# Long convolutions of a three-layer block: tables in two stored parts, the input's factor in the filter, products on VectorE alone, first turning among the last gate tiles

## What is computed

```python
def bidirectional_long_conv(z, h_fwd, h_bwd):
    L, C = h_fwd.shape
    circ = jnp.concatenate([h_fwd, jnp.zeros((1, C), jnp.float32), h_bwd[:0:-1]], axis=0)
    hf = jnp.fft.rfft(circ, axis=0)
    zf = jnp.fft.rfft(z.astype(jnp.float32), n=2 * L, axis=1)
    y = jnp.fft.irfft(zf * hf[None], n=2 * L, axis=1)[:, :L]
    return y.astype(z.dtype)
...
    filters = implicit_filters(S, filt_w1, filt_b1, filt_w2, filt_b2, filt_w3, filt_b3, filt_w4, filt_freq)
    z = v
    for o, gate_o in enumerate((x1, x2)):
        z = gate_o * (bidirectional_long_conv(z, filters[:, o, 0], filters[:, o, 1]) + filt_bias[o] * z)
    y_hy = z * jax.nn.silu(g_hy)
```

## Time and profile before

| what | value |
|---|---|
| three runs | 4669.88, 4673.32, 4674.02 us (median 4673.32) |
| the profiled execution | 4672.72 us, its span 4670.9 us |
| mean granted clock of PE | 0.958 |
| busy share of the span: PE, DVE, ACT, POOL | 90%, 49%, 30%, 5% |
| chain that ended last: PE, DVE, ACT, DMA | 80%, 12%, 4%, 1% |
| last gate tile ends, merge's first matmul | 4125.3 us, 4420.66 us |

### The profile page before, as it was taken

One profiled execution on the slowest core, in us unless ns is written; L12 is line 12 of the kernel. 1 busy time (PEld: TensorE's weight loads), 2 busy tenths in 40 slices (PEclk: granted clock), 3 DMA queues, 4 the chain that ended last, 5 costly groups with the idle time before them and its releaser, 6 DMA issues.

```text
span 4670.9 us, 47189 instructions
## 1 busy us (share of the span) xinstructions
PE 4223.0 (90%) x18908; PEld 3155.9 (68%) x18908; DVE 2277.0 (49%) x3345; ACT 1398.0 (30%) x2292; POOL 231.6 (5%) x205
## 2 busy tenths in 40 slices
PE   6888889899999988889899999959999999987695
PEld 3566555688888766655578888847777777866574
DVE  6677346544343355355533332343445455466645
ACT  2323435322122233335321121123434333122221
POOL 2200000000000000000000000010000000021101
PEclk9999999899999989999899999979999999998897
DMA  4432200132331200200122221111111111122231
GB/s 163 153 111 84 83 14 1 45 99 91 92 98 55 81 28 23 84 14 1 32 77 68 72 68 54 46 63 46 41 46 41 46 41 59 46 90 77 90 135 45
DMA packets 87905, 304.16 MB, mean 65 GB/s; under 512 B 9735, under 2 KB 10535, under 8 KB 86600
## 3 DMA queue, kind: packets, MB, share of 16 engines
q1 hardware_dynamic: 69112, 229.31, 15.1%
q0 software_dynamic: 18576, 71.84, 4.9%
HBM read 266.50 MB, written 34.60 MB: 64 GB/s over the span
## 4 chain that ended last, share of the span: by engine, by line
PE 80%; DVE 12%; ACT 4%; issue 2%; DMA 1%; POOL 0%; SPq 0%; DVEq 0%; ACTq 0%
PE PS L915 54%; PE PS L1774 3%; PE PS L698 2%; PE PS L2793 2%; PE PS L1248 1%; PE PS L1646 1%; PE PS L2207 1%; PE PS L1501 1%; PE PS L1495 1%; PE PS L1675 1%; PE PS L2234 1%; PE PS L1645 1%; PE PS L2220 1%; PE PS L626 1%; DVE WL L471 1%
## 5 line engine op out<-in xcount | busy, mean ns | idle before, releaser
L915 PE MATMUL PS<-hi,WH 128*128 128x512 f32 x2816 | 1170.8, 416 | 111.2 <-issue 37.6
L915 PE MATMUL PS<-lo,WH 128*128 128x512 f32 x2816 | 1131.5, 402 | 0.0
L915 PE MATMUL PS<-hi,WL 128*128 128x512 f32 x2816 | 1126.1, 400 | 0.0
L915 PEld LDWEIGHTS PS<-hi,WH 128*128 128x128 f32 x2816 | 539.3, 192 | 292.2 <-issue 106.0
L915 PEld LDWEIGHTS PS<-hi,WL 128*128 128x128 f32 x2816 | 538.9, 191 | 131.5
L915 PEld LDWEIGHTS PS<-lo,WH 128*128 128x128 f32 x2816 | 540.4, 192 | 120.2 <-issue 5.4
L465 ACT ACTIVATE WH<-raw 128x1024 fp32r<-128x1024 f32 x304 | 319.8, 1052 | 793.4 <-PE PS L915 601.1
L471 DVE TENSOR_TENSOR WL<-raw,WH 128x1024 fp32r<-128x1024 f32 x304 | 391.1, 1287 | 260.6 <-ACT WH L465 260.5
L915 PE MATMUL PS<-al,WH 128*128 128x512 f32 x1024 | 408.6, 399 | 0.0
L915 PE MATMUL PS<-ah,WH 128*128 128x512 f32 x1024 | 403.5, 394 | 0.0
L915 PE MATMUL PS<-ah,WL 128*128 128x512 f32 x1024 | 401.4, 392 | 0.0
(11 more groups left out here) (423 smaller groups left out, 5465.9 us busy)
## 6 DMA issues: line engine op xcount, KB each, us to landing
adab<-in_w_ada POOLq DMA_DIRECT2D x120, 512.0 KB, 4.6
raw<-in_win SPq DMA_DIRECT2D x104, 512.0 KB, 3.6
raw<-in_up SPq DMA_DIRECT2D x64, 512.0 KB, 3.6
raw<-in_down SPq DMA_DIRECT2D x64, 512.0 KB, 3.6
raw<-in_dft SPq DMA_DIRECT2D x24, 512.0 KB, 3.7
sp_x<-X SPq DMA_DIRECT2D x24, 512.0 KB, 6.3
X<-sp_x SPq DMA_DIRECT2D x24, 512.0 KB, 5.4
raw<-in_wout SPq DMA_DIRECT2D x24, 512.0 KB, 3.7
```

Source lines behind the costliest of these rows:

```text
L915: mm = pe.matmul(bank[b + hf], w[:, k, :], r[:, k, HALF[hf]], start=k == 0 and w is wh and r is hi, stop=k == 7 and w is wl)
```

## The change

Code around it is in the kernel's own words, with the lines of the kernel before where there are any.

1. `dft` and `idft` tables lie in HBM as two arrays each, high and low part (`two_parts`, on the host). SP loads both (a second DMA of 512 KB for each of the 40 table tiles), ACT copies both (`WH` and `WL`), and `weights_dve` skips table tiles.
2. `fbias` is added to the filter's value at position 0 (one DMA of 1x1024, two additions of 1x512 on DVE), so L2706 goes away and the gate multiplies the PSUM bank at once.
3. All products and all eight `Yf` rows run on DVE; POOL only loads `cb`. `zc` has one buffer instead of two, `p1` is new.
4. The first turning (`o` = 0) runs on banks 6 and 7 during the last three gate tiles; `zh`, `zl` moved to memory that is free by then. For `o` = 1, four of the eight groups are turned among the tiles of the inverse.
5. The first spectrum block takes both tables' even halves before the odd ones. Inverse and spectrum use other banks, so that each starts without the other's being drained.
6. The merge splits `Yb` before the last inverse has ended.

```diff
-HYENA = rest_at(20) + 10
+HYENA = rest_at(20)
+SPECTRUM = 6.3
+ORDER = 98.5
 def turned_at(o, nt):
-    return HYENA + 175 * o + 1.5 * nt
+    if o == 0:
+        return rest_at(17) + 4 * nt
+    return inverse_at(0, 1, nt + 1) + 0.6 if nt < 4 else HYENA + ORDER + (3.0 if nt < 6 else 5.75) + 0.4 * (nt % 2)
...
-MERGE = HYENA + 360
+MERGE = inverse_at(1, 1, 4)
...
                 sp.dma_start(halves(to) if key[0] == "wout" else to, source(key)).then_inc(*W_RAW[j % 2].next(j, by=16))
+                if is_table(j):
+                    to, src = table_low(j)
+                    if j > 7 and not is_table(j - 2):
+                        sp.wait_ge(*DA_DVE["pair", 3])
+                        sp.wait_ge(*GH_OUT[1][71])
+                    sp.dma_start(to[:, :], src).then_inc(*W_RAW[j % 2].next(j, by=16))
...
                 act.activation(WH[:, j % 2, :], raw[:, j % 2, :], ACT.Copy).then_inc(*W_HI.next(j))
+                if is_table(j):
+                    act.activation(WL[:, j % 2, :], table_low(j)[0][:, :], ACT.Copy).then_inc(*W_TABLE.next(j))
...
             for j in range(len(WEIGHTS)):
+                if is_table(j):
+                    continue
...
                         dve.tensor_tensor(m.ft[0:1, o, :], PS[0:1, 6 + o, :], m.dec[0:1, 0, :],
-                                          ALU.mult).then_inc(*FI_DVE.next("value", (0, 0, o)))
+                                          ALU.mult).then_inc(*FI_DVE.next("middle", o))
+                        dve.wait_ge(*FI_DVE["middle", o])
+                        dve.wait_ge(*FBIAS_IN[0])
+                        dve.tensor_tensor(m.ft[0:1, o, :], m.ft[0:1, o, :], m.fso[0:1, 0, o, :],
+                                          ALU.add).then_inc(*FI_DVE.next("value", (0, 0, o)))
...
-                    pool.tensor_tensor(PROD, z0, csn, ALU.mult).then_inc(*HY_POOL.next("cross", o, mt))
...
+                    dve.tensor_tensor(m.p1[:, :, :], z1, imag, ALU.mult).then_inc(*HY_DVE.next("minus", (o, mt)))
+                    dve.tensor_tensor(m.p2[:, :, :], z0, imag, ALU.mult).then_inc(*HY_DVE.next("cross", (o, mt)))
...
-                        dve.scalar_tensor_tensor(out=zp, in0=zp, scalar=vc("fbias", 4 * o + ct), in1=bank[4 * par + ct],
-                                                 op0=ALU.mult, op1=ALU.add).then_inc(*HY_DVE.next("biased", o, par, ct))
-                        dve.wait_ge(*HY_DVE["biased", o, par, ct])
-                        dve.tensor_tensor(zp, zp, gp, ALU.mult).then_inc(*HY_DVE.next("filtered", o, par, ct))
+                        dve.tensor_tensor(zp, bank[inverse_bank(o, par, ct)], gp, ALU.mult).then_inc(
+                            *HY_DVE.next("filtered", o, par, ct))
...
+def two_parts(table):
+    part, power = np.frexp(table)
+    high = np.ldexp(np.round(part * 2048) / 2048, power)
+    return np.stack([high, table - high]).astype(np.float32)
```

More of the change, by code:

```diff
@@ L537, in setup_sp @@
             sp.dma_start(m.w4[:, :, :, :].rearrange("p a b c -> p (a b c)"), D["fw4"]).then_inc(*W4_IN.next(0, by=16))
+            sp.dma_start(m.fso[0:1, 0, :, :], D["fbias"]).then_inc(*FBIAS_IN.next(0, by=16))
             yield 2.0
@@ L2514, in turned_pe @@
                             pe.wait_ge(*RE_DVE["conv", 4 + i])
+                        pe.wait_ge(*DA_ACT["out", 11, 1])
+                        pe.wait_ge(*DA_DVE["turned", BLOCKS - 1])
                     if o:
                         pe.wait_ge(*HY_DVE["filtered", 0, par, 3])
-                    if nt % 4 > 1:
+                    if nt % 4 > 1 or nt > 3 and not o:
                         pe.wait_ge(*HY_DVE["low", o, nt - 2])
[L2519 to L2522, removed]
                     for ct in range(4):
@@ L2535, in turned_act @@
                     elif nt == 0:
-                        act.wait_ge(*W_MM[TILE_OF["win2", 55][0]])
-                        act.wait_ge(*RE_DVE["gate", 19, 1])
+                        act.wait_ge(*RE_DVE["conv", 15])
+                        act.wait_ge(*DA_DVE["pair", 3])
+                        for hf in range(2):
+                            act.wait_ge(*GH_OUT[hf][71])
                     act.activation(m.zh[:, nt, :], bank[turned_bank(o, nt)], ACT.Copy).then_inc(
@@ L2550, in spectrum_pe @@
             for o in range(2):
[L2551 to L2576, removed]
@@ new lines, in spectrum_pe @@
+                order = [(0, cs, par) for par in range(2) for cs in range(2)]
+                order += [(mt, cs, par) for mt in range(1, 4) for cs in range(2) for par in range(2)]
+                for i, (mt, cs, par) in enumerate(order):
+                    j = TILE_OF["dft", cs, mt][1 + o]
+                    wh, wl = weight_tile(j)
+                    b = bank[spectrum_bank(o, cs, par)]
+                    for n4 in range(4):
+                        nt = 4 * par + n4
+                        yield HYENA + ORDER * o + SPECTRUM / 2 * (i + n4 / 4)
+                        if mt == 0 and cs == 0:
+                            pe.wait_ge(*HY_DVE["low", o, nt])
+                        if nt == 0:
+                            pe.wait_ge(*W_TABLE[j])
+                        if n4 == 0:
+                            if mt:
+                                pe.wait_ge(*(HY_DVE["sum", o, mt - 1, cs] if par else HY_ACT["even", o, mt - 1, cs]))
+                            elif o == 0:
+                                pe.wait_ge(*(HY_DVE["low", 0, 6 + par] if cs else DA_ACT["spread sums", 11, 2]))
+                            else:
+                                pe.wait_ge(*(HY_DVE["filtered", 0, 0, 2 + par] if cs else HY_DVE["low", 1, 2 + par]))
+                        for w, r in ((wh, m.zh), (wh, m.zl), (wl, m.zh)):
+                            mm = pe.matmul(b, w[:, nt, :], r[:, nt, :], start=n4 == 0 and w is wh and r is m.zh,
+                                           stop=n4 == 3 and w is wl)
+                        if mt == 3 and cs == 1:
+                            mm.then_inc(*W_MM.next(j, nt))
+                            W_MM.at[j,] = W_MM.n
+                        elif nt == 7:
+                            mm.then_inc(*W_MM.next(j))
@@ L2587, in spectrum_act @@
                             act.wait_ge(*HY_DVE["sum", 0, 3, cs])
-                        act.activation(EVEN[cs], bank[2 * cs], ACT.Copy).then_inc(*HY_ACT.next("even", o, mt, cs))
+                        else:
+                            act.wait_ge(*RE_DVE["gate", 19, 1])
+                        act.activation(EVEN[cs], bank[spectrum_bank(o, cs, 0)], ACT.Copy).then_inc(
+                            *HY_ACT.next("even", o, mt, cs))
         def spectrum_dve(dve):
```

199 lines of the change are left out of this document (102 added, 97 removed).

## The result

| | us |
|---|---|
| before, median of 4 runs | 4673.7 (4669.9 to 4675.1) |
| changed, median of 4 runs | 4531.9 (4530.2 to 4549.5) |
| ratio, 95% interval | 0.9706 [0.9682, 0.9731] |
| forecast | 4582, range 4568 to 4602 |

What follows compares the result with a forecast made beforehand. PE was taken to bound the gate tiles, and DVE to set the pace from there to the merge. Start -5.3, transposes +4.5, convolutions -87.1 and merge -2.5 sum to -90.4: 4672.7 becomes 4582.3 us, range 4568 to 4602.

Steps and rivals of the forecast that it cites:

- third sine piece: Program start: DVE's third sine piece starts at 22.3 to 22.7 instead of 28.83; with +0.8 for the second addition, net -5.3.
- transposes among the gate tiles: First turning: 32 transposes go among the gate tiles, where PE is the bound, +4.5 us.
- block of DVE: Spectrum: DVE's load per block is 12.0 us against PE's 11.2, so DVE sets the pace.
- stop between the halves: Inverse: PE waits 3.25 us instead of 6.37, with DVE's filter still ahead of the odd half's split.
- merge's start: After both orders the merge starts 208.2 us after the last gate tile's end, where 295.3 stood: -87.1.
- merge: Merge: 384 matmuls go on without a stop, 89.5 us instead of 92.27, entered as -2.5.
- T itself: T is the end of the last gate tile; start (-5.3) and transposes (+4.5) were to move it by -0.8 us.
- The rest of the two first layers is in the same order and moves along: Layers between start and gates: order unchanged, so they only shift with the start, at no cost or gain of their own.
- Tables that come late (1): Spectrum: transfers one after another take 15.3 us per block, not 12.0; +26, 4608 us; chance 0.10.
- load and copy in turn (3): Table tiles: load and copy don't overlap, 9.3 us for each of 32 tiles; 4685 us, slower than before; chance 0.02.
- `cb` held back (2): Spectra: `cb`'s load moves only in DVE's pauses, so third and fourth blocks wait 5.7 us; +23, 4605; chance 0.04.
- The turning was hidden (4): Gate tiles: the rival said the turning isn't hidden, transposes and splits delaying them another 10 us; 4593; chance 0.05.

Runs made afterwards that it cites:

- a_gap32: The changed kernel with 32 unused bytes per partition behind `col`, so the tiles both kernels have stand at the old addresses: 4584.6 us.
- a_gap192: The changed kernel with 192 unused bytes per partition behind `col`, so layers' moving and stationary tiles begin alike modulo 256: 4515.9 us.
- a_wh64: The changed kernel with 64 unused bytes ahead of `WH` and 192 behind `WL`, so stationary tiles begin like the moving ones modulo 256: 4513.2 us.
- b_wh32: The kernel before with 32 unused bytes ahead of `WH` and 224 behind `WL`; moving tiles keep their place modulo 256: 4638.1 us.
- e_turn2: The changed kernel with the first turning put behind the last gate tile again: 4553.8 us.
- b_gap32: The kernel before with 32 unused bytes per partition behind `col`: 4669.3 us.
- b_gap160: The kernel before with 160 unused bytes per partition behind `col`, so layers' moving and stationary tiles begin alike modulo 256: 4618.9 us.
- b_gap96: The kernel before with 96 unused bytes per partition behind `col`: 4676.2 us.

## Why the prediction was wrong, point by point

| step | forecast | trace of the changed kernel |
|---|---|---|
| third sine piece | 22.3 to 22.7 | 22.68 |
| transposes among the gate tiles | +4.5 | +3.8 (8 x 0.47) |
| block of DVE | 12.0 | 12.00 |
| inverse's start | T+49.7 | T+49.1 |
| stop between the halves | 3.25 | 3.2 |
| first order's end | T+103.6 | T+102.0 |
| merge's start | T+208.2 | T+205.8 |
| merge | 89.5 | 87.99 |
| stop before `wout2` | stays | 4.88 (4.89) |
| T itself | -0.8 | -47.3 |

**The step that failed** is the half sentence that costs everything between the start and the gates' end at nothing: "The rest of the two first layers is in the same order and moves along." The order is the same; the pace is not. The term that was missing is the number of untouched matmuls times the change of their period, 11,136 x 0.0044, less what is not PE-bound: 44 us ahead of T, and 3 to 4 in merge and `wout2` (90.70 to 88.84 there). The rest of the miss: the start gave 6.8 us (the first layer's first matmul at 204.6 for 211.4) where 5.3 were set, and the convolutions 2.3 more than was forecast, of which 1.6 are the place again (a_gap32 takes 207.6 from the last gate matmul to the merge, the changed kernel 206.0). In the start, the second addition's +0.8 didn't reach PE: its third group of the filter's products begins at 51.24 for 57.38 us, all of the sine layers' 6.1. And the merge's term should have been -2.8 by its own numbers (92.27 less 89.5), not -2.5.

In a_gap32's profile, at the old places, the terms are near one by one: the start 5.4 us (5.3), the transposes 3.7 (4.5), the convolutions 87.8 (87.1), the merge 2.7 (2.5). That the whole median then meets the forecast by 2 us is partly luck, since its runs lie at 4581.4 to 4592.8.

The range failed for the same reason. Its bounds were worked out for each step, and the common factor, the 0.233 us per matmul that some 12,000 instructions share, had none. A change of 2% in that number outweighs all the bounds together.

**The rivals.** Tables that come late (1) and load and copy in turn (3) did not occur: DMA shares rose (0.56 over the stretch from T to the merge, 197 GB/s), a `cb` took 6.8 us in place of 5.1 and a second part 4.7 to 5.7, but nothing waited for them. `cb` held back (2) did not occur. The turning was hidden (4). The stop between the halves ends as was forecast. The chain above goes back to ACT's copy of a table's second part, but leaves 1.11 us of "issue" behind it. The timeline (start, duration) shows what PE, which waits for the first `zl` of the half, waited for in them:

```profile
4151.71 2.49 DVE L2749 TENSOR_TENSOR X<-PS,X 128x512 f32<-128x512 f32 x4 [7.28 <-PE PS L2778]
4152.73 1.04 ACT L500 ACTIVATE WL<-tl 128x1024 fp32r<-128x1024 f32 x1
4154.11 2.49 DVE L2740 TENSOR_TENSOR zl<-Yf,zh 128x512 fp32r<-128x512 f32 x4
4154.90 0.77 PE L2776 MATMUL PS<-WH,zh 128*128 128x512 f32 x1 [3.22 <-issue]
```

ACT is done at 4153.8. DVE goes from its four gate multiplications to the first `zl` at 4154.1 and, at 0.68 us for one, ends it at 4154.8; PE starts 0.1 us later. The Trainium skill's rule that was weighed against the rows (VectorE: DVE Perf Modes, section The DRAIN you can't avoid), full DVE durations, would have given blocks of 12.8 us; the trace has 12.00 and starts 1.14 us apart. The same section lets an instruction that isn't held start earlier, and that is what the trace shows.

## What to carry to other kernels

Before a change is costed, compare where the tiles lie, not the order of instructions alone: a constant that leaves a small tile shifts all that is laid out behind it. Where thousands of like matmuls bound the kernel, try the places of moving and stationary tiles against each other in steps of 32 bytes; here equal starts modulo 256 took 0.2265 us per matmul, the changed kernel's place 0.2287 and the worst 0.2332. Equal starts are worth 16 to 19 us on top of this change (a_gap192 4515.9, a_wh64 4513.2, the fastest of all), for unused tiles of 192 or 256 bytes per partition. When a time comes out well and unforeseen, put the old layout under the new work before crediting the work.

## What was not expected of the hardware

**The period of a matmul depends on D.** All are 128x512 fp32r matmuls, stationary 128x128, at a granted clock of 1.00. What in the chip makes it was not tried. That it hangs on the distance of the two tiles, and not on either's own place or on the work beside it, is shown for D = 0 and 64 (b_wh32, a_wh64). The other places are one position each of the stationary tiles. It isn't the chip: the kernel before ran beside each group of runs and had medians of 4673.4 to 4676.1. The Trainium skill (TensorE: Matmul & The Clock Gate, section Part 2: What happens when you issue a matmul) gives 0.216 us from start to start for 512 columns, without a figure for fp32r; no stretch here comes below 0.226, and the page doesn't speak of places.

**D doesn't settle it wholly.** In e_turn2's profiled run, D = 64, the first layer's MLP ran at the slow pace and the second's at the fast one:

```profile
922.06 708.12 PE PS L958 x3027
2347.34 693.13 PE PS L958 x3027
```

Fifteen us go there. b_gap32 shows the same between 2145 and 2154 per 500 us. A stretch seems to keep the pace with which it began; what chooses it is open.

**The clock rises at another moment in each profile, and the filter stage varies by some 12 us with it.** The profile of e_turn2 has, in its first filter tile, groups of six matmuls in 2.86 us until 84 us (chain of waits):

```profile
61.66 2.86 PE PS L741 x6
64.51 3.71 PE PS L664 x4
...
84.21 3.71 PE PS L664 x4
87.92 8.29 PE PS L741 x24
```

In the changed kernel's profile only the first group does:

```profile
61.85 2.86 PE PS L741 x6
64.70 2.37 PE PS L664 x4
67.07 1.59 PE PS L741 x6
```

2.86 for six is the pace of 1.2 GHz, 1.59 that of 2.4. The windows print PEclk 1.00 over all of this, but they have nothing to go by: the trace's first record of the granted clock begins only at 65.6 us in the changed kernel, at 70.6 in before, 93.4 in e_turn2, 97.8 in b_gap160 and 99.6 and 100.7 in b_gap96 and b_gap32. In each of the sixteen profiles PE's matmuls of 512 columns first start less than 0.3 us apart within 3 us of that record. So the record marks the rise, and ahead of it PE ran at the lower level. The filter's last matmuls come at 186 us in the changed kernel's profile, at 193 in before, at 199 in e_turn2 and at 204 to 207 in the three with the latest rise. What decides when the clock rises was not tried. Such a 1.00 at the start of a trace should be checked against the distance of the matmuls.
